# Attention probabilities and values in two float32r parts: three products for one float32 product

## The reference

```python
logits = jnp.einsum('bqgrd,bqkgd->bqgrk', q_b, k_sel).astype(jnp.float32) * att_scale
logits = jnp.where(valid[:, :, None, None, :], logits, NEG_INF)
p = jax.nn.softmax(logits, axis=-1)
return jnp.einsum('bqgrk,bqkgd->bqgrd', p.astype(v.dtype), v_sel)
```

## Time and profile before

| what | value |
|---|---|
| median of 3 runs | 3548.53 us (3545.34 to 3552.7) |
| profiled execution: its time / its span in the trace | 3548.37 us / 3546.8 us |
| mean granted clock of PE in it | 0.937 of full speed |
| busy share of the span | PE 85%, weight load 63%, DVE 70%, ACT 52%, POOL 13% |
| attention stage: first exponential to last value product | 1271 to 1945 us of the span |
| costliest groups of that stage | L2156 PE 287.6 us, L2335 DVE 185.7 us, L2117 PE 193.2 us, L2307 ACT 160.5 us |

### The profile page before, as it was taken

The page is one execution under the profiler, slowest core; times in us unless marked ns, Lnnn a source line. Parts: engine busy times, 40 slices in busy tenths (PEclk is TensorE's granted clock), DMA queues, the critical chain, the costliest instruction groups (busy, mean ns, idle before and its releaser), DMA issues. The chain is left out here.

```text
span 3546.8 us, 45365 instructions
## 1 busy us (share of the span) xinstructions
PE 3000.0 (85%) x12950; PEld 2229.5 (63%) x12950; DVE 2476.3 (70%) x3895; ACT 1835.2 (52%) x2532; POOL 473.5 (13%) x618
## 2 busy tenths in 40 slices
PE   2898699899999968998899599993499999999970
PEld 2675478678678734555454478772377777777750
DVE  4467588789989956776642444443489988988964
ACT  6222357578578534443433233330477777777750
POOL 0111100000000042212111000002211111111113
PEclk8999899999999979999999799996799999999985
DMA  2122322122212274444322555641479779666869
GB/s 106 59 73 72 102 74 81 64 66 80 73 60 75 69 173 133 111 108 97 90 63 52 176 180 168 184 123 40 150 259 351 280 289 350 220 252 241 311 231 379
DMA packets 369763, 537.73 MB, mean 152 GB/s; under 512 B 37428, under 2 KB 202836, under 8 KB 369492
## 3 DMA queue, kind: packets, MB, share of 16 engines
q1 hardware_dynamic: 339300, 431.39, 38.6%
q0 software_dynamic: 28016, 96.18, 7.4%
q10 hardware_dynamic: 2304, 8.39, 0.6%
HBM read 510.54 MB, written 130.18 MB: 181 GB/s over the span
## 5 line engine op out<-in xcount | busy, mean ns | idle before, releaser
L898 DVE TENSOR_TENSOR e_w_lo<-e_raw,e_w_hi 128x1024 fp32r<-128x1024 f32 x392 | 452.9, 1218 | 0.0
L1577 PE MATMUL x_ps<-h_hi,x_w_hi 128*128 128x512 f32 (+1 forms) x1024 | 401.8, 392 | 0.0
L1577 PE MATMUL x_ps<-h_lo,x_w_hi 128*128 128x512 f32 (+1 forms) x1024 | 400.9, 391 | 0.0
L1577 PE MATMUL x_ps<-h_hi,x_w_lo 128*128 128x512 f32 (+1 forms) x1024 | 400.7, 391 | 0.0
L850 ACT CAST e_w_hi<-e_raw 128x1024 fp32r<-128x1024 f32 x392 | 382.0, 1049 | 0.7 <-PE e_pG L801 0.7
L1767 DVE TENSOR_SCALAR_CACHE_REDUCE x_relu<-x_score,x_cand 128x1024 uint8<-128x1024 f32 (+3 forms) x217 | 315.6, 1487 | 3.6
L1680 ACT ACTIVATE x_relu<-x_score,x_cand 128x896 int8<-128x896 f32 (+3 forms) x217 | 281.0, 1296 | 55.8 <-DVE x_cand L1774 55.5
L2335 DVE CUSTOM_DVE_ANT_0 t_junk<-t_L,t_mask 128x512 bf16<-128x512 f32 (+3 forms) x320 | 185.7, 607 | 163.0 <-PE t_L L2117 162.0
L2156 PE MATMUL t_O<-t_probT,t_v 128*65 128x512 f32 x544 | 287.6, 611 | 13.7 <-ACT t_probT L2307 12.3
L2307 ACT ACTIVATE t_probT<-t_ST 128x512 f32<-128x512 f32 x272 | 160.5, 593 | 257.6 <-PE t_ST L2148 257.0
L801 PE MATMUL e_pG<-e_w_hi,e_x_hi 128*128 128x512 f32 x768 | 246.6, 402 | 4.3 <-DVE e_w_lo L898 3.6
(11 more groups left out here) (391 smaller groups left out, 6222.1 us busy)
## 6 DMA issues: line engine op xcount, KB each, us to landing
e_raw<-in_w_exp_gate SPq DMA_DIRECT2D x392, 256.0 KB
e_raw<-in_w_exp_up SPq DMA_DIRECT2D x392, 256.0 KB
e_raw<-in_w_exp_down SPq DMA_DIRECT2D x192, 512.0 KB
projT<-x_out SPq DMA_DIRECT2D x124, 256.0 KB, 2.7
slot_out<-e_y POOLq DMA_DIRECT2D x48, 512.0 KB
o_gate<-projT SPq DMA_DIRECT2D x32, 512.0 KB, 5.0
x_w_raw<-in_w_in SPq DMA_DIRECT2D x31, 512.0 KB
x_t<-in_x SPq DMA_DIRECT2D x16, 512.0 KB
```

What stands on the lines that cost most here:

```text
L898: nc.vector.tensor_tensor(w_lo[:, u, :], raw[:, u, :], w_hi[:, u, :].bitcast(F32), ALU.subtract).then_inc(gl, 1)
L1577: last = nc.tensor.matmul(ps[0:w, u % 4, :], wt[:, m % 2, kk, 0:w], ht[:, kk, q * 512:(q + 1) * 512], start=(kk == 0 and s == 0), stop=(kk ...
```

## The change

`PT` by `V` in float32 is replaced by three products of float32r operands (a rounded format of 32 bits): high probabilities by high values, high probabilities by low values, low probabilities by high values. `PH` (high) is a second exponential written in float32r, `PL` (low) is `PT - PH` on DVE, `V_hi` and `V_lo` are made once on POOL, a quarter (4 key blocks) at a time.

```diff
+        V_hi, V_lo = sb("v_hi", [P, NT, AKV, AD + 1], F32R), sb("v_lo", [P, NT, AKV, AD + 1], F32R)
-        PT, OU = sb("probT", [P, 3, 512]), sb("out", [AD + 1, 3, R4, P])
+        PT, PH, PL, OU = sb("probT", [P, 2, 512]), sb("prob_hi", [P, 3, 512], F32R), sb("prob_lo", [P, 3, 512], F32R), sb("out", [AD + 1, 2, R4, P])
...
 # POOL
+            def split(q):
+                part = slice(4 * q, 4 * q + 4)
+                pool.wait_ge(v_in[q], 16)
+                g.tensor_copy(V_hi[:, part, :, :], V[:, part, :, :]).then_inc(vh_ok, 1)
+                pool.wait_ge(vh_ok, q + 1)
+                g.tensor_tensor(V_lo[:, part, :, :], V[:, part, :, :], V_hi[:, part, :, :].bitcast(F32), ALU.subtract).then_inc(vl_ok, 1)
...
             pool.wait_ge(row_ok, 1)
+            split(0)
             for s in range(AHEAD):
                 diagonal(s)
...
                     side(FIRST[s] + j)
+                if s in (1, 5, 9):
+                    split((s + 3) // 4)
                 if s + AHEAD < len(STEPS):
                     diagonal(s + AHEAD)
...
 # PE, values(s, j)
+                f = FIRST[s] + j
                 pe.wait_ge(p_ok, at_st[s, j] + 1)
                 if j == 0 and s:
                     pe.wait_ge(ou_ok, s)
-                nc.tensor.matmul(O[0:AD + 1, :, :], V[:, j, v, :], PT[:, (FIRST[s] + j) % 3, :], start=(j == 0), stop=(j == n)).then_inc(pv_ok, 1)
+                if n == j and j % 4 == 0 and v == 0:
+                    pe.wait_ge(vl_ok, j // 4 + 1)
+                o = O[0:AD + 1, :, :]
+                nc.tensor.matmul(o, V_hi[:, j, v, :], PH[:, f % 3, :], start=(j == 0), stop=False)
+                nc.tensor.matmul(o, V_lo[:, j, v, :], PH[:, f % 3, :], start=False, stop=False)
+                pe.wait_ge(pl_ok, f + 1)
+                nc.tensor.matmul(o, V_hi[:, j, v, :], PL[:, f % 3, :], start=False, stop=(j == n)).then_inc(pv_ok, 1)
...
 # ACT, each block
                     if f >= 3:
                         act.wait_ge(pv_ok, f - 2)
-                    a.activation(PT[:, f % 3, :], ST[:, u % 2, :], ACT.Exp).then_inc(p_ok, 1)
+                    if f >= 2:
+                        act.wait_ge(pl_ok, f - 1)
+                    a.activation(PT[:, f % 2, :], ST[:, u % 2, :], ACT.Exp).then_inc(pf_ok, 1)
+                    a.activation(PH[:, f % 3, :], ST[:, u % 2, :], ACT.Exp).then_inc(p_ok, 1)
...
 # DVE
+            def low(f):
+                dve.wait_ge(p_ok, at_p[f] + 1)
+                dve.wait_ge(pf_ok, f + 1)
+                if f >= 3:
+                    dve.wait_ge(pv_ok, f - 2)
+                v_.tensor_tensor(PL[:, f % 3, :], PT[:, f % 2, :], PH[:, f % 3, :].bitcast(F32), ALU.subtract).then_inc(pl_ok, 1)
...
                 for j in range(n + 1):
                     while x < due(s, j):
                         maximum(s + AHEAD, x, seen)
                         seen, x = seen + 1, x + 1
                     if j == n and s + AHEAD < len(STEPS):
                         negated(s + AHEAD, seen)
+                    low(FIRST[s] + j)
                     side(FIRST[s] + j)
```

More of the change, by code:

```diff
@@ L1835, in attend_and_recur @@
                 at_nm[s + 1], at = at, at + 1
+    at_p = [at_st[s, j] for s, (n, _) in enumerate(STEPS) for j in range(n + 1)]
     def parts(n):
@@ L1895, in attend_and_recur @@
         mk_in = [sem(f"mask_in{b}") for b in range(4)]
-        y_st = [sem(f"y_stored{b}") for b in range(3)]
+        y_st = [sem(f"y_stored{b}") for b in range(2)]
         mk_set, l_ok, mx_ok, nm_ok, d_ok, st_ok, p_ok, pv_ok, ou_ok = (sem(n) for n in (
             "mask_set", "l_ok", "mx_ok", "nm_ok", "d_ok", "st_ok", "p_ok", "pv_ok", "out_ok"))
+        pf_ok, pl_ok, vh_ok, vl_ok = sem("p_full"), sem("p_lo_ok"), sem("v_hi_ok"), sem("v_lo_ok")
         g_in, g_w, g_ex, g_tr, g_ev, g_dma, own_s = (sem("g_" + n) for n in ("in", "w", "ex", "tr", "ev", "dma", "own"))
@@ L2015, in store @@
                     sp.dma_start(y_d[k * AD:(k + 1) * AD, 2 * v:2 * v + 2, n * P:(n + 1) * P],
-                                 OU[0:AD, s % 3, k::2, :]).then_inc(y_st[s % 3], 16)
-                sp.dma_start(sum_d[v * R4:(v + 1) * R4, n * P:(n + 1) * P].rearrange("(o h) n -> o h n", o=1), OU[AD:AD + 1, s % 3, :, :]
-                             ).then_inc(y_st[s % 3], 16)
+                                 OU[0:AD, s % 2, k::2, :]).then_inc(y_st[s % 2], 16)
+                sp.dma_start(sum_d[v * R4:(v + 1) * R4, n * P:(n + 1) * P].rearrange("(o h) n -> o h n", o=1), OU[AD:AD + 1, s % 2, :, :]
+                             ).then_inc(y_st[s % 2], 16)
             for f in range(FLAT + 20):
@@ L2026, in _ @@
                 side(f)
-            for b in range(3):
-                sp.wait_ge(y_st[b], 48 * len(range(b, len(STEPS), 3)))
+            for b in range(2):
+                sp.wait_ge(y_st[b], 48 * len(range(b, len(STEPS), 2)))
             for b in range(2):
@@ L2140, in logits_t @@
                 if n == j and j % 4 == 0 and v == 0:
-                    pe.wait_ge(v_in[j // 4], 16)
                     if j == 4:
@@ L2296, in out @@
                 act.wait_ge(pv_ok, FIRST[s + 1])
-                if s >= 3:
-                    act.wait_ge(y_st[s % 3], 48 * (s // 3))
-                a.copy(OU[:, s % 3, :, :], O[0:AD + 1, :, :]).then_inc(ou_ok, 1)
+                if s >= 2:
+                    act.wait_ge(y_st[s % 2], 48 * (s // 2))
+                a.copy(OU[:, s % 2, :, :], O[0:AD + 1, :, :]).then_inc(ou_ok, 1)
             shift_row(0)
```

## The result

The changed kernel took 3656.82 us (median of 4 runs, 3648.74 to 3662.19) against 3549.17 us before: a ratio of 1.0302, 95% interval 1.0278 to 1.0325. It is **slower by 107 us**; the forecast was slower, 3643 us in a range of 3580 to 3720.

What follows compares the result with a forecast made beforehand. It took the attention stage's first stretch as bound by no single engine and the second by PE. From 3548.4 us, +90 for the first and +5 for the second gave 3643 us, range 3580 to 3720.

Steps and rivals of the forecast that it cites:

- the first stretch: Attention stage, steps 0 to 27, 212 blocks with logits and maxima: from 560 us to 660, taken as +90 after overlaps.
- the second: Attention stage, steps 28 to 31, 60 blocks without logits, bound by PE: from 114 us to 119, +5.
- the ring: Per block: subtraction, third value product, next logits, their maxima, next subtraction, each waiting in turn; 2.39 us without sides.
- The split of the values at the start: POOL's first high and low values hide behind PE's 16 logit products: nothing, at most 3 us.
- would just fit: First stretch: the subtraction adds 146 us to DVE, together 528 of 560 us, which alone would fit.
- DVE never makes PE wait: Rival: subtractions come as early as PE wants them and PE gives back 49 us, about 3500 us; chance 0.05.
- PE's 49 us: Value products: three at 0.23 us instead of 0.87 relieve PE by 0.18 us a block, 49 us over 272 blocks.
- excess of the sides: First stretch: DVE's side operations, such as convolution taps, lengthen blocks by what exceeds the 0.84 us gap: 103 us.
- The overlap of 0.08 us: DVE instructions start 0.08 us before the last has drained, which takes 17 us off the first stretch.
- a PE side counts half: Second stretch: two blocks share a PE side, so some 6 us a chunk count as 12 us in four chunks.
- 20 us were put down for it: First stretch: a quarter of the subtractions wait 0.4 us for POOL on the shared SBUF port, 20 us.
- a case of its own: Rival: PE's short waits bring half clock in every second block, 95 us more, 3740 us; chance 0.12.

Runs made afterwards that it cites:

- e3: Changed kernel with the third product taking the high probabilities, so PE does not wait for the subtraction; all work kept; 3608.27 us.
- e7: e2 plus the second exponential and a subtraction on unchanging operands, with none of the change's new waits; 3607.31 us.
- e6: e2 plus one subtraction per block in DVE's list on unchanging operands, waiting for nobody and awaited by nobody; 3593.13 us.
- e2: Changed kernel with only the three products: no second exponential, no subtraction, the third product taking the high probabilities again; 3539.48 us.
- e1: Changed kernel with the subtraction of a block ahead of that block's maxima on DVE, not behind them; 3629.61 us.
- e8: Changed kernel with the subtraction ahead of the maxima on DVE and value products two blocks behind the transposed logits instead of one; 3625.19 us.
- e12: e6 with its subtraction replaced by a reduction of the same length that reads one SBUF operand instead of two; 3570.08 us.
- e5: e2 plus the second exponential, whose result nobody uses, without any subtraction; 3555.25 us.
- e11: Changed kernel with the subtraction moved from DVE to POOL ahead of its side, and value products two blocks behind; 3634.0 us.

## Why the prediction was right, and where it was not

**The sum.** By the windows, the first stretch was forecast at +90 us and measured at +99, the second at +5 and +15. The total came out at 3657 against 3643, in the direction and well inside the range.

**The blocks' terms.** Value products: 0.23 us apart, as forecast. Subtraction: 0.69 at the median. Second exponential: 0.59. The turn of the ring: 2.07 against 2.13. A block of the first stretch: 659 / 212 = 3.11 us, as forecast. PE's wait for the subtraction's line: 145 us, over the 80 named. DVE busy in the first stretch: 78%, over the 75% named. A block of the second stretch: 129.4 / 60 = 2.16 us, over the 1.95 named. The split of the values at the start: first exponential 1273.3 us against 1271.1, 2 us by that comparison, where nothing was forecast with 3 as the bound.

**Where the cause was misjudged.** The forecast said that the ring makes the loss and that otherwise DVE's sum, 528 of 560 us, "would just fit". The runs show it does not. Laid out from the kernel before:

- three products: -11
- second exponential: +15
- subtraction in DVE's list, tied to nobody: +53 (some 15 of it by its second operand); with the exponential +69
- PE's wait for it (e3 to the changed kernel): +48

That is -11 + 69 + 48 = 106 of 107 us. So the ring's wait, added last, is the smaller part. The step that failed is the sentence "That alone would just fit" and, with it, the price of the rival "DVE never makes PE wait": it was 3500 us, and e3 and e7, in which DVE makes no value product wait, took 3608 and 3607. Two of its terms were off. DVE's free time is not free: the subtraction costs 53 us even untied, and the waits of e6 show others that stand for the end of DVE's longer rows. And PE's 49 us gave only 11 back: before and in e2, PE is busy 606 and 575 us of the stage, 31 us less, and idle 68 and 86, 18 us more. That the sum came out near was in part luck. It put the whole loss on a ring that turns in every block, and PE waited for the subtraction in 126 of 212. It may have come out because the ring counted DVE's work in full, subtraction and excess of the sides, and that work costs with the ring and without it; this is a reading, and no run shows it.

**A term misread.** The overlap of 0.08 us was taken from 0.69 of record against 0.60, but that 0.60 is the mean busy time of maxima of all sizes. The turn above shows the right comparison: a full maximum starts at 1504.42 and the next instruction of its length at 1505.04, 0.62 apart. That makes 15 us of the 17.

**The mending that the ring promised** gave little: e1 and e8 loosened the ring and left 79 and 73 of 107 us. The work costs without the ring too (e7: 58 us), and both runs let DVE wait longer for exponentials.

**The second stretch** was off by 10 us. Third value products of the changed kernel there:

```profile
2036.92 0.45 PE L2176 MATMUL t_O<-t_prob_lo,t_v_hi 128*65 128x512 f32 x1
2038.39 0.45 PE L2176 MATMUL t_O<-t_prob_lo,t_v_hi 128*65 128x512 f32 x1
2041.62 0.39 PE L2176 MATMUL t_O<-t_prob_lo,t_v_hi 128*65 128x512 f32 x1
2043.22 0.44 PE L2176 MATMUL t_O<-t_prob_lo,t_v_hi 128*65 128x512 f32 x1
2045.43 0.44 PE L2176 MATMUL t_O<-t_prob_lo,t_v_hi 128*65 128x512 f32 x1
2048.04 0.45 PE L2176 MATMUL t_O<-t_prob_lo,t_v_hi 128*65 128x512 f32 x1
2051.21 0.45 PE L2176 MATMUL t_O<-t_prob_lo,t_v_hi 128*65 128x512 f32 x1 [1.57 <-DVE t_prob_lo L2366]
```

The blocks without a side at its start take 1.47 and 1.60 us, near the 1.62 of the forecast. But the block with PE's side of offset 6 takes 3.23 (2038.39 to 2041.62), and so it does in all four chunks (3.22 or 3.23): the side counts in full and not by half. The term "a PE side counts half" was wrong. PE's sides sum to some 5.5 us a chunk here, 22 us in four chunks where 12 were put down, and these 10 us are what the stretch was off by. The three blocks up to 2051.21, beside DVE's sides of offsets 8 and 9, take 8.0 us, 3.2 more than three blocks do elsewhere; 0.8 of that is PE's own side of offset 9, and 2.4 are left for DVE's, where 2 were put down.

**POOL.** 20 us were put down for it. All subtractions of the changed kernel (shortest, median, longest in ns):

```profile
L2366 DVE TENSOR_TENSOR t_prob_lo<-t_probT,t_prob_hi x272: 676/688/1768, 1276.2 to 2058.6; 128x512 fp32r<-128x512 f32 x136
```

Their mean is 725 ns over a median of 688, 10 us in 272, and the longest waited 1.1 us; e12 gives 15 us for two operands instead of one in the whole stage, POOL's own delays with it. The term is of the right size as a whole; the subtraction's own waits are half of it.

**The clock** fell in the first stretch to 0.90, which the forecast named as the edge to a case of its own. Over 1271 to 1820 us it is 0.92 in e2, 0.91 in e5 and 0.89 in e6, e7 and e3, so it fell without the ring. From e2 to e6 PE's busy time grew by 25 us of the stage's 58, and some 19 of these would follow from the clocks alone, by the estimate above. What the clock has in the idle time, and whether it fell because of the waits, was not tried and stays open.

## What to carry to other kernels

Before adding an operation to an engine that is busy 70% of a stretch, look at who waits for it, not at the free 30%: where other lists wait for the end of its longer rows of work, close to a third of the new time shows (551 to 598 us, 47 of 146 us, in the first stretch here), even if nobody waits for the new operation itself. If moreover another engine must wait for it, write down the way from its end back to its next start through all lists; that gave the stage's time within 3% here (674 + 95 = 769 us against 788), in part by luck. To learn which of the two costs, run the work once without the wait, on operands that never change, and the wait's price falls out as the difference.

## What the runs showed of the hardware that was not expected

An operation of POOL that nobody changed (the diagonals, 693 ns) grew to 778 ns where DVE's added operations read two SBUF operands, and took 677 ns where they read one. (The one-operand operation is a reduction and so differs in kind too.) The other way round, DVE's taps grew from 780 to 1055 ns in e11, where POOL subtracts, and maxima that read PSUM did not grow at all. And the subtraction on POOL, in e11, took 1323 ns at the mean where DVE takes 690 ns, as its row there shows:

```profile
L2069 POOL TENSOR_TENSOR t_prob_lo<-t_probT,t_prob_hi 128x512 fp32r<-128x512 f32 x272 | 358.0, 1323 | 193.3 <-ACT t_prob_hi L2339 191.4
```

It loaded POOL with 358 us, and that run's attention stage (762 us) was longer than e1's (745) and e8's (752), which left the subtraction on DVE.
